# The convolution's output gate as products of summed blocks, in pairs of tiles next to other tiles

## The chip, the cores and the metric

One core of a Trainium2 chip runs the whole program. The metric is the device time of one launch in microseconds (us), the median of several runs. The engines are TensorE (PE; its weight loads, PEld, overlap the matmuls), VectorE (DVE), ScalarE (ACT), GpSimd (POOL) and SyncE (SP, which issues the DMAs). Each works through a queue of its own in order and waits for the others by semaphores.

## The reference

Two transformer blocks follow each other on a sequence of 512 positions with 1024 features. The second has two layers of mixer, cross-attention and MLP; the mixer of its layer 1 is the part that changes:

```python
def odd_mixer(h, w_in, conv_w, w_out):
    S = h.shape[1]
    proj = h @ w_in
    b_gate = proj[..., :CONV_DIM]
    c_gate = proj[..., CONV_DIM:2 * CONV_DIM]
    z = c_gate * proj[..., 2 * CONV_DIM:]
    zp = jnp.pad(z, ((0, 0), (CONV_WIDTH - 1, 0), (0, 0)))
    y = zp[:, 0:S] * conv_w[0]
    for tap in range(1, CONV_WIDTH):
        y = y + zp[:, tap:tap + S] * conv_w[tap]
    return (b_gate * y) @ w_out
...
h = h + odd_mixer(rms_norm(h, norm_mix_g[l]), conv_w_in[i], conv_w[i], conv_w_out[i])
h = h + cross_attention(rms_norm(h, norm_xattn_g[l]), mem_n, ...)
h = h + sq_relu_mlp(rms_norm(h, norm_mlp_g[l]), mlp_w1[l], mlp_w2[l])
```

CONV_DIM is 1024 and CONV_WIDTH 3; h is 512 × 1024, w_in 1024 × 3072, all float32.

## The kernel before, in words

**Layout.** Activations lie with features on the 128 partitions, eight tiles of 128 × 512 for 1024 features. A float32 matmul runs as three matmuls of type fp32r on a high and a low part of each factor (hi·hi, hi·lo, lo·hi: L2118, L2119, L2120). `t_P0H` and `t_P0L` are the parts of the normed input h, `t_P1H` and `t_P1L` those of a stage's second factor, `t_X` the residual stream.

**Weights** come in chunks of 512 KB into four buffers `t_raw`, in the order of a plan. For each chunk ACT writes the high part `t_whi` (four buffers, L2261) and DVE the low part `t_wlo` (three, L2434). A buffer `t_raw` is fetched anew once its low part is done.

**Order.** `schedule()` writes one list of steps, and each engine's program takes its own steps from it in that order; nothing is reordered later. `later()` puts a low part off to the end of the next tile (`flush()`). `row_end()` closes a norm: it splits the summed squares (DVE L2510), adds them up by a matmul with ones (PE L2200, L2201, behind the first tile of the next stage) and takes the reciprocal root (DVE L2513).

**A plain tile** (`gemm_fm`) makes 128 output columns from one chunk: 8 row blocks × 3 matmuls × 512 columns, 24 matmuls into one PSUM bank.

**The convolution** (functions `ev_c`, `ev_x`, `ev_b` in `schedule()`) runs, for m from 0 to 7, a tile of c_gate, of the third part x and of b_gate, 24 plain tiles in all. DVE evacuates them: conv_c multiplies by the squared row of the norm (L2844), conv_x multiplies in x (L2850) and runs the three taps (L2853, L2855, L2858), conv_b multiplies by the row (L2866), conv_out gates (L2869); then the product is split into P1 (ACT L2299, DVE L2490). `conv_w_out` follows as eight tiles (`mixed`), whose k-th row block needs P1's k-th tile.

**The seven products.** MLP 0 before it makes its first factor in pairs of tiles (`mlp`, `pair_of_tiles`). A pair takes two chunks as 2 × 2 blocks of 4 × 128 rows, and the input as 2 × 2 blocks of 4 row blocks × 256 columns; by the Strassen-Winograd form seven products of summed blocks give the four output blocks. A product is 4 row blocks × 3 matmuls × 256 columns. The sums of activations `T1` to `T4` are made by `combine` (a gain on ACT L2273, four DVE instructions L2455, L2456, L2459, L2462, then a split) and lie in `t_E3`; those of weights by `sums` (DVE L2444, L2445, L2447, L2449), S1 in `t_Tb`, its parts in `t_PTbR`. `Parts` splits such chunks (ACT L2268, DVE L2439). In the functions of a pair `low` writes a low part and asks for the next chunk into that buffer, `next_to` the high part of a neighbour's weights, `other` runs the neighbour's tile. `product` keeps PSUM running across products, `snap` copies a bank to SBUF (ACT L2278), `c_add` adds a bank to it (DVE L2467). Between the products stand plain tiles of a neighbour, whose weights are split into `t_MH`, `t_ML` (two pairs of buffers), while the pair's own chunks wait in `t_raw`.

Of the kernel before, what the change touches and what calls it, by code (L numbers as in the profile page):

```python
# [158 lines left out]
def schedule(T, A, plan, apart=()):  # L159
# [1791 lines left out]
    squared = [False]
    for m in range(8):
        box = {}

        def ev_c(bank, p):
            if not squared[0]:
                emit("row_squared", dst=R2, row=N.row)
                squared[0] = True
            t, free = TMP.take()
            box["t"], box["id"] = t, emit("conv_c", t=t, bank=bank, p=p, r2=R2, free=free).id  # L1960
            return "conv_c", box["id"]

        def ev_x(bank, p, m=m):
            zb = UP[:, m % 2, :]
            emit("conv_x", t=box["t"], bank=bank, p=p, z=zb[:, 16:528],
                 taps=[(zb[:, 16 - k:528 - k], gcol(f"cw{2 - k}", m)) for k in range(3)])
            return "conv_x", box["id"]
# [456 lines left out]
def vector_program(e, steps, at, mark, T):  # L2424
# [4 lines left out]
    for s in steps:  # L2429
# [408 lines left out]
        elif s.name == "conv_c":  # L2838
            for k in s.free:
                e.wait_ge(*at(*k))  # L2840
# [3 lines left out]
            e.tensor_tensor(s.t, s.bank, s.r2, ALU.mult).then_inc(*mark("conv_c", s.id))  # L2844
        elif s.name == "conv_x":
            if new(("conv_zero", 0)):
                e.wait_ge(*at("conv_zero"))
            e.wait_ge(*at("conv_c", s.id))
# [1 line left out]
            e.tensor_tensor(s.z, s.bank, s.t, ALU.mult).then_inc(*mark("conv_x", s.id))  # L2850
            e.wait_ge(*at("conv_x", s.id))
# [1 line left out]
            e.tensor_scalar(s.t, z2, c2, None, ALU.mult, ALU.bypass).then_inc(*mark("tap2", s.id))  # L2853
            e.wait_ge(*at("tap2", s.id))
            e.scalar_tensor_tensor(out=s.t, in0=z1, scalar=c1, in1=s.t, op0=ALU.mult,  # L2855
                                   op1=ALU.add).then_inc(*mark("tap1", s.id))
            e.wait_ge(*at("tap1", s.id))
            e.scalar_tensor_tensor(out=s.t, in0=z0, scalar=c0, in1=s.t, op0=ALU.mult,  # L2858
                                   op1=ALU.add).then_inc(*mark("tap0", s.id))
        elif s.name == "conv_b":  # L2860
            for k in s.free:
                e.wait_ge(*at(*k))
# [2 lines left out]
            e.wait_ge(*at(*s.p))
            e.tensor_tensor(s.s, s.bank, RB[:, :], ALU.mult).then_inc(*mark("conv_b", s.id))  # L2866
            e.wait_ge(*at("conv_b", s.id))
            e.wait_ge(*at("tap0", s.id))
            e.tensor_tensor(s.s, s.s, s.t, ALU.mult).then_inc(*mark("conv_out", s.id))  # L2869
# [212 lines left out]
```

## Time and profile before

| | us |
|---|---|
| median of 3 runs | 2223.2 (2221.88 to 2223.98) |
| the profiled execution | 2222.34, span 2220.3 |
| PE busy | 2199.0 (99%) |
| DVE busy | 1454.9 (66%) |
| ACT busy | 975.7 (44%) |
| granted PE clock, mean | 0.999 of full speed |

The span runs from the first to the last instruction that the profiler saw; 2.0 us of the execution lie around it. The window 1577 to 1705 us is the convolution, MLP 0 ends just before it. In a row of a timeline "128x512 f32<-128x512 f32" is the shape written and read, and a bracket gives the engine's idle time before the instruction and what ended it. An instruction's duration can be longer than the step to the next one, since an engine starts the next while one drains.

### The profile page before, as it was taken

The numbers are of one execution on the slowest core, as the hardware profiler recorded it, in microseconds if no ns is written. First come the engines' busy times: TensorE is split into PE (matmuls) and PEld (weight loads), VectorE is DVE, ScalarE is ACT, GpSimd is POOL, SyncE is SP. The second block draws the span as 40 slices with busy tenths as digits, with TensorE's granted clock in tenths as the row PEclk, the third lists the DMA queues.
The fourth block names the chain that finished last, engine by engine and source line by source line (L and its number), as shares of the span: only waits on it lengthen the run. The fifth ranks groups of instructions, "written<-read, shape, count | busy, mean of one in ns | idle before, by whom it ended". The sixth has DMA issues, their size and how long they took to land.

```text
span 2220.3 us, 31738 instructions
## 1 busy us (share of the span) xinstructions
PE 2199.0 (99%) x12112; PEld 1860.7 (84%) x12112; DVE 1454.9 (66%) x2448; ACT 975.7 (44%) x1676; POOL 14.5 (1%) x14
## 2 busy tenths in 40 slices
PE   9999999999999999999999999999999999999998
PEld 7877788888778888888898889998888888899997
DVE  5866565557656567686665777776755657776775
ACT  5445533334445334364553544443322435444444
POOL 0000000000000000200000000000000000000000
PEclk9999999999999999999999999999999999999999
DMA  5565443335644333465354333333233213233331
GB/s 201 164 186 156 146 129 109 104 125 180 185 135 152 116 101 115 125 176 147 114 154 132 95 95 96 114 96 105 88 99 96 89 48 105 88 102 97 99 112 55
DMA packets 136694, 268.14 MB, mean 121 GB/s; under 512 B 21773, under 2 KB 79931, under 8 KB 136160
## 3 DMA queue, kind: packets, MB, share of 16 engines
q1 hardware_dynamic: 136544, 266.13, 39.3%
...
## 4 chain that ended last, share of the span: by engine, by line
PE 70%; DVE 3%; ACT 1%; issue 1%; DMA 1%; POOL 1%; SPq 0%; DVEq 0%; POOLq 0%; ACTq 0%
PE ps L2118 22%; PE ps L2120 22%; PE ps L2119 22%; PE ps L2146 1%; PE ps L2135 1%; DVE t_wlo L2434 1%; POOL t_UP L2101 1%; DMA far<-t_UP 0%; DVE t_UP L2694 0%; PE ps L2170 0%; DVE t_Tb L2662 0%; PE ps L2158 0%; PE ps L2160 0%; PE ps L2159 0%; PE ps L2172 0%
## 5 line engine op out<-in xcount | busy, mean ns | idle before, releaser
L2118 PE MATMUL ps<-t_P0H,t_whi 128*128 128x512 f32 (+1 forms) x1568 | 590.6, 377 | 3.8 <-DVE t_P0L L2479 1.9
L2119 PE MATMUL ps<-t_P0L,t_whi 128*128 128x512 f32 (+1 forms) x1568 | 584.4, 373 | 0.0
L2120 PE MATMUL ps<-t_P0H,t_wlo 128*128 128x512 f32 (+1 forms) x1464 | 552.8, 378 | 0.0
L2434 DVE TENSOR_TENSOR t_wlo<-t_raw,t_whi 128x1024 fp32r<-128x1024 f32 (+2 forms) x289 | 342.7, 1186 | 44.7 <-PE ps L2120 32.2
L2261 ACT ACTIVATE t_whi<-t_raw 128x1024 fp32r<-128x1024 f32 (+2 forms) x295 | 300.8, 1025 | 153.6 <-PE ps L2120 152.1
L2118 PEld LDWEIGHTS ps<-t_P0H,t_whi 128*128 128x128 f32 x1568 | 295.2, 188 | 73.1 <-issue 16.4
L2119 PEld LDWEIGHTS ps<-t_P0L,t_whi 128*128 128x128 f32 x1568 | 294.9, 188 | 56.2 <-issue 1.0
L2120 PEld LDWEIGHTS ps<-t_P0H,t_wlo 128*128 128x128 f32 x1464 | 275.2, 188 | 54.7
L2118 PE MATMUL ps<-t_P1H,t_whi 128*128 128x512 f32 (+1 forms) x548 | 210.0, 383 | 1.6 <-DVE t_P1L L2819 1.0
L2119 PE MATMUL ps<-t_P1L,t_whi 128*128 128x512 f32 (+1 forms) x548 | 208.5, 380 | 0.0
L2120 PE MATMUL ps<-t_P1H,t_wlo 128*128 128x512 f32 (+1 forms) x524 | 201.1, 384 | 0.0
L2119 PE MATMUL ps<-t_P1L,t_MH 128*128 128x512 f32 x384 | 150.7, 393 | 0.0
L2120 PE MATMUL ps<-t_P1H,t_ML 128*128 128x512 f32 x384 | 150.6, 392 | 0.0
L2118 PE MATMUL ps<-t_P1H,t_MH 128*128 128x512 f32 x384 | 150.2, 391 | 0.0
L2831 DVE TENSOR_TENSOR t_X<-ps,t_X 128x512 f32<-128x512 f32 (+1 forms) x136 | 88.8, 655 | 74.0 <-PE ps L2120 73.9
L2268 ACT ACTIVATE t_whi<-t_raw 128x1024 fp32r<-128x1024 f32 x72 | 75.8, 1055 | 109.4 <-DVE t_raw L2449 109.4
L2118 PEld LDWEIGHTS ps<-t_P1H,t_whi 128*128 128x128 f32 x548 | 103.2, 188 | 22.9 <-DVE t_P1L L2819 1.2
L2119 PEld LDWEIGHTS ps<-t_P1L,t_whi 128*128 128x128 f32 x548 | 103.1, 188 | 20.8 <-issue 0.2
L2120 PEld LDWEIGHTS ps<-t_P1H,t_wlo 128*128 128x128 f32 x524 | 98.4, 188 | 20.9
L2414 ACT ACTIVATE t_TMP<-t_TMP 128x512 f32<-128x512 f32 x64 | 40.2, 628 | 136.6 <-DVE t_TMP L2827 136.6
L2287 ACT ACTIVATE t_P0H<-t_X,t_gv 128x512 fp32r<-128x512 f32 x56 | 40.3, 725 | 113.7 <-DVE t_X L2600 100.7
L2342 ACT ACTIVATE t_Tb<-t_Tb,t_ST 128x128 f32<-128x128 f32 (+3 forms) x96 | 51.6, 539 | 86.7 <-DVE t_ST L2670 73.0
...
## 6 DMA issues: line engine op xcount, KB each, us to landing
...
```

Source lines behind the costliest of these rows:

```text
L2101: e.tensor_tensor(dst, a, b, ALU.add).then_inc(*mark("window", (s.g, i)))
L2118: e.matmul(s.out, s.sh, s.mh, start=s.first, stop=False, skip_group_check=again)
L2119: e.matmul(s.out, s.sh, s.ml, start=False, stop=False, skip_group_check=again)
L2120: i = e.matmul(s.out, s.sl, s.mh, start=False, stop=s.end, skip_group_check=again)
L2135: i = e.matmul(bank[:, o:o + n], q, k, start=True, stop=True)
L2261: e.activation(s.dst, s.raw, ACT.Copy).then_inc(*mark("hi", s.j))
L2268: e.activation(s.hi, s.src, ACT.Copy).then_inc(*mark("part_hi", s.id))
L2287: e.activation(s.dst, s.src, ACT.Copy, scale=s.col).then_inc(*mark("norm_hi", s.id))
L2342: i = e.activation(t[:, o:o + n], t[:, o:o + n], ACT.Exp, bias=s.s[:, 4 + c + k:5 + c + k], accum_out=s.s[:, 8 + c + k:9 + c + k])
L2414: e.activation(s.t, s.t, ACT.Square).then_inc(*mark("relu_square", s.id))
L2434: e.tensor_tensor(s.dst, s.raw, s.hi.bitcast(F32), ALU.subtract).then_inc(*mark("lo", s.j))
L2831: e.tensor_tensor(s.x, s.bank, s.x, ALU.add).then_inc(*mark("add_x", s.id))
```

## The change

The eight b_gate tiles become four pairs of seven products, and the order of the convolution is written anew. Six plain tiles come first (c0, x0, c1, x1, c2, x2). Next to the pairs stand the other ten: c3, x3, c4 in pair 0, x4, c5, x5 in pair 1, c6, x6 in pair 2, c7, x7 in pair 3. Within a pair the order on PE is: B11, B21, the first neighbour, T2, T3, the second neighbour if there are three, T1, the last neighbour, B22, T4. The sums of activations are made from the end of MLP 0 on: sum 0 and 1 around its last two tiles, 2 and 3 between plain tiles. The convolved y(m) waits in the places of `t_P1L` (`t_QKV` lies over them) until `gate_out` multiplies it into a snapshot in SBUF. The last pair gives its buffers back to `conv_w_out`'s weights.

The core of the diff:

```diff
         if l == 0:
-            run(second(7))
+            tread[0] = "product", prods[0] - 1
+            for m in range(8):
+                if m % 2 == 0:
+                    w = Weight(chunk("mlp_w2", l, halves(512 * 7, 4), halves(128 * m, 2)))
+                run(second_tile(7, m, w, m % 2))
+                combine(*{5: ["gain 0", "gain 1"], 6: ["add 0"], 7: ["high 0", "add 1"]}.get(m, []))
...
-        def ev_b(bank, p, m=m):
-            s, free = TMP.take()
-            emit("conv_b", s=s, t=box["t"], bank=bank, p=p, free=free, row=N.row)
-            TMP.give(box["t"], ("conv_out", m))
-            split_into(P1, m, s, ("conv_out", m), give=s)
-            return "conv_b", m
-
-        for base, ev in ((1024, ev_c), (2048, ev_x), (0, ev_b)):
-            w = Weight(chunk("conv_w_in", 0, halves(0), halves(base + 128 * m, 1)))
-            run(gemm_fm(P0, w, parts8(), ev))
...
+        def gate_out(m, t, after):
+            emit("conv_b", m=m, s=t, t=y(m), after=after, row=N.row)
+            split_into(P1, m, t, ("conv_out", m), give=t)
...
+        kinds = {"c": (1024, gate_in), "x": (2048, taken_in)}
+        first = [("c", 0), ("x", 0), ("c", 1), ("x", 1), ("c", 2), ("x", 2)]
+        beside = [[("c", 3), ("x", 3), ("c", 4)], [("x", 4), ("c", 5), ("x", 5)], [("c", 6), ("x", 6)],
+                  [("c", 7), ("x", 7)]]
+        wf = [Weight(w_in(kinds[g][0], m)) for g, m in first]
...
+        def next_to(q, i):
+            if not dry and q < 4 and i < len(beside[q]):
+                U[q][f"w{i}"] = Parts(raw_of(B[q, i]), [landed(B[q, i])], MHs, MLs)
+
+        def low(q, name, of=None):
+            if not dry and name in U[q]:
+                key = U[q][name].rest()
+                if of is not None:
+                    fetch(of + NRAW, key)
+
+        def other(q, i):
+            g, m = beside[q][i]
+            run(gemm_fm(P0, U[q][f"w{i}"], parts8(), kinds[g][1](m)))
+
+        def plain(i, *work):
+            g, m = first[i]
+            run(gemm_fm(P0, wf[i], parts8(), kinds[g][1](m)))
+            combine(*work)
+
+        plain(0, "low 0", "high 1", "gain 2")
+        plain(1, "low 1", "add 2", "gain 3")
+        plain(2, "high 2", "add 3")
+        plain(3, "low 2", "high 3")
+        u0(0)
+        plain(4, "low 3")
+        low(0, "u0")
+        sums(0)
+        u12(0, 0)
+        plain(5)
+        low(0, "u1", A[0][0])
+        u12(0, 1)
+        low(0, "u2", A[0][1])
+        next_to(0, 0)
+        u3(0)
+        low(0, "w0", B[0, 0])
...
+            p = product(bx, u["u0"], 0, "B11", True, xf)
+            s1 = snap(a0, p, af)
+            if q == 0:
+                low(0, "u3")
+            next_to(q, 1)
+            p = product(bz, u["u0"], 4, "B21", True, zf)
+            u["u0"].done(p)
+            c11 = add(a0, z, s1, p)
+            PB.give(bz, c11)
+            low(q, "w1", B[q, 1])
+            other(q, 0)
+            if more:
+                u0(q + 1)
+            else:
+                ahead(W["n"] - 1)
+            p = product(bx, u["u1"], 0, "T2", False, [s1])
+            s2 = snap(b0, p, bf)
+            low(q + 1, "u0")
+            p7 = product(bv, u["u2"], 0, "T3", True, vf)
+            sums(q + 1)
+            if three:
+                next_to(q, 2)
+                other(q, 1)
+                low(q, "w2", B[q, 2])
+            u12(q + 1, 0)
+            if not more:
+                ahead(W["n"] - 1)
+            p = product(bx, u["u3"], 0, "T1", False, [s2])
+            u["u3"].done(p)
+            U[4]["S1"] = p
+            s3 = snap(b1, p)
+            c22 = add(b1, v, s3, p7)
+            low(q + 1, "u1", A[q + 1][0] if more else None)
+            other(q, 2 if three else 1)
+            next_to(q + 1, 0)
+            u3(q + 1)
+            p = product(bx, u["u1"], 4, "B22", False, [s3])
+            u["u1"].done(p)
+            c12 = snap(a1, p)
+            PB.give(bx, c12)
+            u12(q + 1, 1)
+            gate_out(2 * q, tA, [c11, c12])
+            if not more:
+                ahead(W["n"] - 1)
+            p = product(bv, u["u2"], 4, "T4", False, [c22])
+            u["u2"].done(p)
+            c21 = add(b0, v, s2, p)
+            PB.give(bv, c21)
+            low(q + 1, "u3")
+            low(q + 1, "w0", B[q + 1, 0] if more else None)
+            low(q + 1, "u2", A[q + 1][1] if more else None)
+            gate_out(2 * q + 1, tB, [c22, c21])
```

Below stand the places in the listing of DVE's and PE's instructions on which the prediction rests. A row names the line, the operation, what it writes from what it reads, and the semaphores it waits on. In the changed kernel every line of the programs stands 210 lower (L2434 is L2644, L2439 is L2649, L2200 is L2410).

The first place is DVE around the last residual add of MLP 0 (`t_X`) and the split of the summed squares (`t_P1L<-t_SQ,t_P1H`); `t_E_85` is `t_E3` with the sums of activations. Before:

```order
L2831 TENSOR_TENSOR t_X<-ps,t_X 128x512 [waits s_mm]
L2479 SCALAR_TENSOR_TENSOR t_P0L<-t_X,t_gv,t_P0H 128x512 [waits s_norm_hi]
L2487 TENSOR_TENSOR t_SQ<-t_SQ,t_TMP 128x512 [waits s_add_square,s_square]
L2833 MEMSET t_UP 128x2x16
L2434 TENSOR_TENSOR t_wlo<-t_raw,t_whi 128x1024 [waits s_mm,s_hi]
L2510 TENSOR_TENSOR t_P1L<-t_SQ,t_P1H 128x512 [waits s_norms_act]
```

and in the change:

```order
L3041 TENSOR_TENSOR t_X<-ps,t_X 128x512 [waits s_mm]
L2665 TENSOR_TENSOR t_E_85<-t_TMP 128x256 [waits s_parts_act,s_product]
L2666 SCALAR_TENSOR_TENSOR t_E_85<-t_X,t_gv,t_TMP 128x256
L2669 SCALAR_TENSOR_TENSOR t_E_85<-t_X,t_gv,t_E_85 128x256 [waits s_parts_dve]
L2672 SCALAR_TENSOR_TENSOR t_E_85<-t_X,t_gv,t_E_85 128x256 [waits s_parts_dve]
L2689 SCALAR_TENSOR_TENSOR t_P0L<-t_X,t_gv,t_P0H 128x512 [waits s_norm_hi]
L2697 TENSOR_TENSOR t_SQ<-t_SQ,t_TMP 128x512 [waits s_add_square,s_square]
L3043 MEMSET t_UP 128x2x16
L2644 TENSOR_TENSOR t_wlo<-t_raw,t_whi 128x1024 [waits s_mm,s_hi]
L2720 TENSOR_TENSOR t_P1L<-t_SQ,t_P1H 128x512 [waits s_norms_act]
```

Four instructions came in behind this residual add, and the same four behind the one before it.

The second place is DVE at the end of the sixth plain tile, x2, whose conv_x is L3058; the first tile next to pair 0, c3, reads `t_ML` (before, b_gate's tile came behind such a conv_x, and DVE's next row was an ordinary low part):

```order
L3058 TENSOR_TENSOR t_UP<-ps,t_QKV 128x512 [waits s_mm,s_conv_dve]
L3061 TENSOR_SCALAR t_QKV<-t_UP,t_gv 128x512 [waits s_conv_dve]
L3063 SCALAR_TENSOR_TENSOR t_QKV<-t_UP,t_gv,t_QKV 128x512 [waits s_conv_dve]
L3066 SCALAR_TENSOR_TENSOR t_QKV<-t_UP,t_gv,t_QKV 128x512 [waits s_conv_dve]
L2649 TENSOR_TENSOR t_TbR<-t_raw,t_whi 128x1024 [waits s_parts_act,s_mm]
L2649 TENSOR_TENSOR t_wlo<-t_raw,t_whi 128x1024 [waits s_parts_act,s_mm]
L2649 TENSOR_TENSOR t_ML<-t_raw,t_MH 128x1024 [waits s_mm,s_parts_act]
L2649 TENSOR_TENSOR t_PTbR<-t_Tb,t_PTbR 128x512 [waits s_parts_act,s_product]
L2677 TENSOR_TENSOR t_TMP<-t_TMP,ps 128x256 [waits s_product,s_parts_act]
```

The low part of c3's weights, `t_ML`, stands behind conv_x with its taps and two other low parts.

The third place is DVE in pair 0 behind the tile x3, with the low part for c4 (`t_ML`):

```order
L2659 TENSOR_TENSOR t_raw<-t_raw 128x512 [waits s_parts_dve]
L3058 TENSOR_TENSOR t_UP<-ps,t_QKV 128x512 [waits s_mm,s_conv_dve]
L3061 TENSOR_SCALAR t_QKV<-t_UP,t_gv 128x512 [waits s_conv_dve]
L3063 SCALAR_TENSOR_TENSOR t_QKV<-t_UP,t_gv,t_QKV 128x512 [waits s_conv_dve]
L3066 SCALAR_TENSOR_TENSOR t_QKV<-t_UP,t_gv,t_QKV 128x512 [waits s_conv_dve]
L2649 TENSOR_TENSOR t_ML<-t_raw,t_MH 128x1024 [waits s_parts_act,s_mm]
L2677 TENSOR_TENSOR t_TMP<-t_TMP,ps 128x256 [waits s_product,s_parts_act]
L2649 TENSOR_TENSOR t_wlo<-t_raw,t_whi 128x1024 [waits s_parts_act,s_product]
L3052 TENSOR_TENSOR t_QKV<-ps,t_UP 128x512 [waits s_mm]
```

It stands behind x3's conv_x. PE asks for both low parts at a tile's first matmul; between the end of x2 and c3's first matmul it has two products. Of PE's rows there, the last of B21 and the first three of c3:

```order
L2328 MATMUL ps<-t_P0H,t_whi 128x256
L2329 MATMUL ps<-t_P0L,t_whi 128x256
L2330 MATMUL ps<-t_P0H,t_wlo 128x256
L2328 MATMUL ps<-t_P0H,t_MH 128x512 [waits s_parts_dve,s_conv_dve]
L2329 MATMUL ps<-t_P0L,t_MH 128x512
L2330 MATMUL ps<-t_P0H,t_ML 128x512
```

Before, PE's next row behind a conv_x tile was the first of a gate tile, with 512 columns from `t_whi`.

## Rows read from the trace of the kernel before

**Rows 1.** The head of the page: span, busy time of each engine

```profile
span 2220.3 us, 31738 instructions
PE 2199.0 (99%) x12112; PEld 1860.7 (84%) x12112; DVE 1454.9 (66%) x2448; ACT 975.7 (44%) x1676; POOL 14.5 (1%) x14
```

**Rows 2.** Windows: us, then busy us (instructions) by engine, PEclk, DMA share, GB/s

```profile
940.00:944.00 4.00, 2.12 (x12) 1.55 (x12) 3.65 (x16) 2.89 (x10) 0.00 (x0) 1.00 0.07 19
1491.20:1512.20 21.00, 21.00 (x135) 18.96 (x134) 15.11 (x23) 9.10 (x14) 0.00 (x0) 1.00 0.36 102
1577.00:1705.00 128.00, 128.00 (x554) 103.87 (x553) 71.02 (x86) 28.64 (x31) 0.00 (x0) 1.00 0.31 95
...
2213.80:2215.30 1.50, 0.00 (x0) 0.00 (x0) 1.42 (x2) 0.00 (x0) 0.00 (x0) 0.97 0.00 0
2215.30:2220.00 4.70, 0.00 (x0) 0.00 (x0) 1.00 (x2) 0.00 (x0) 0.00 (x0) 0.50 0.65 225
```

**Rows 3.** Timeline of PE in MLP 0: start us, us, line, operation, out<-in

```profile
1307.15 0.28 PE L2118 MATMUL ps<-t_P0H,t_whi 128*128 128x256 f32 x1
...
1309.98 0.39 PE L2118 MATMUL ps<-t_P1H,t_MH 128*128 128x512 f32 x1
```

**Rows 4.** Timeline of DVE at the end of MLP 0

```profile
1569.10 0.68 DVE L2831 TENSOR_TENSOR t_X<-ps,t_X 128x512 f32<-128x512 f32 x1
1570.57 0.75 DVE L2479 SCALAR_TENSOR_TENSOR t_P0L<-t_X,t_gv,t_P0H 128x512 fp32r<-128x512 f32 x1 [0.79 <-ACT t_P0H L2287]
1571.24 0.69 DVE L2487 TENSOR_TENSOR t_SQ<-t_SQ,t_TMP 128x512 f32<-128x512 f32 x1
1571.85 0.68 DVE L2831 TENSOR_TENSOR t_X<-ps,t_X 128x512 f32<-128x512 f32 x1
...
1574.63 1.19 DVE L2434 TENSOR_TENSOR t_wlo<-t_raw,t_whi 128x1024 fp32r<-128x1024 f32 x1
1575.74 0.69 DVE L2510 TENSOR_TENSOR t_P1L<-t_SQ,t_P1H 128x512 fp32r<-128x512 f32 x1
```

**Rows 5.** Timeline of DVE, one sum of activations ahead of MLP 0

```profile
1225.29 0.42 DVE L2455 TENSOR_TENSOR t_E<-t_TMP 128x256 f32<-128x256 f32 x1
1225.62 0.48 DVE L2456 SCALAR_TENSOR_TENSOR t_E<-t_X,t_gv,t_TMP 128x256 f32<-128x256 f32 x1
...
1226.94 1.22 DVE L2434 TENSOR_TENSOR t_wlo<-t_raw,t_whi 128x1024 fp32r<-128x1024 f32 x1
```

**Rows 6.** Timeline of DVE in the convolution: conv_x and its taps, conv_b, conv_out

```profile
1583.10 0.69 DVE L2850 TENSOR_TENSOR t_UP<-ps,t_TMP 128x512 f32<-128x512 f32 x1
...
1585.81 1.22 DVE L2434 TENSOR_TENSOR t_wlo<-t_raw,t_whi 128x1024 fp32r<-128x1024 f32 x1
1588.63 0.69 DVE L2866 TENSOR_TENSOR t_TMP<-ps,t_RB 128x512 f32<-128x512 f32 x1 [1.61 <-PE ps L2120]
1589.36 0.69 DVE L2869 TENSOR_TENSOR t_TMP<-t_TMP 128x512 f32<-128x512 f32 x1
```

**Rows 7.** Timeline of DVE, low parts of weights in MLP 0

```profile
1302.36 1.22 DVE L2439 TENSOR_TENSOR t_ML<-t_raw,t_MH 128x1024 fp32r<-128x1024 f32 x1
1303.49 0.69 DVE L2439 TENSOR_TENSOR t_PTbR<-t_Tb,t_PTbR 128x512 fp32r<-128x512 f32 x1
```

**Rows 8.** Timeline of PE, the first matmul behind that gate tile

```profile
1588.36 0.39 PE L2118 MATMUL ps<-t_P0H,t_whi 128*128 128x512 f32 x1
```

**Rows 9.** Timeline of all engines, PE going on after a wait for DVE

```profile
1043.68 0.69 DVE L2600 SCALAR_TENSOR_TENSOR t_X<-ps,t_X 128x512 f32<-128x512 f32 x1
...
1044.42 0.50 PE L2118 MATMUL ps<-t_P1H,t_whi 128*128 128x512 f32 x1 [0.60 <-DVE t_X L2600]
...
1044.76 0.39 PE L2119 MATMUL ps<-t_P1L,t_whi 128*128 128x512 f32 x1
```

**Rows 10.** Timeline of PE, the row sum after the first convolution tile

```profile
1576.75 0.39 PE L2200 MATMUL ps<-t_P1H,t_ones 128*128 128x512 f32 x1
```

**Rows 11.** Timeline of ACT, a snapshot of a product in MLP 0

```profile
1303.17 0.39 ACT L2278 ACTIVATE t_TMP<-ps 128x256 f32<-128x256 f32 x1 [2.57 <-PE ps L2120]
```

More of the change, by code:

```diff
@@ L1641, in combine @@
                 emit("combine", t=u.t, of=u.id, x=X[:, k + 4, :], col=gcol(u.gain, k + 4), T=both,
-                     read=("x_values", ids["x_values"]))
+                     read=tread[0])
                 TMP.give(u.t, ("combined", u.id))
@@ L1942, in n1 @@
         norm_tile(m, o, "mix1", P0, sqa)
+        if m > 3:
+            tsum[m - 4] = Rec(gain="mix1", x=o)
     mlp(0, n1)
     row_end()
-    R2 = E3[:, 8, :]
+    R2 = UP[:, 2, 0:512]
     emit("conv_zero", dst=UP[:, 0:2, 0:16])
[L1951 to L1967, printed above, removed]
-        def ev_b(bank, p, m=m):
-            s, free = TMP.take()
-            emit("conv_b", s=s, t=box["t"], bank=bank, p=p, free=free, row=N.row)
-            TMP.give(box["t"], ("conv_out", m))
-            split_into(P1, m, s, ("conv_out", m), give=s)
-            return "conv_b", m
-        for base, ev in ((1024, ev_c), (2048, ev_x), (0, ev_b)):
-            w = Weight(chunk("conv_w_in", 0, halves(0), halves(base + 128 * m, 1)))
-            run(gemm_fm(P0, w, parts8(), ev))
@@ L1979, in schedule @@
+    conv()
     flush()
-    cuts = split_kv(1, [k for _, f in blocks.idle + grouped.idle + turned.idle for k in f])
+    cuts = split_kv(1, [k for _, f in blocks.idle + grouped.idle + turned.idle for k in f] +
+                    ([] if dry else [("product", prods[0] - 1)]))
     for n, _ in enumerate(mixed("conv_w_out", 0, halves(0), 1.0, "xa1", P1)):
@@ L2847, in vector_program @@
                 e.wait_ge(*at("conv_zero"))
[L2848 removed]
+            e.wait_ge(*at("conv_c", s.m))
             e.wait_ge(*at(*s.p))
[L2850 to L2851 removed]
+            e.tensor_tensor(s.z, s.bank, s.t, ALU.mult).then_inc(*mark("conv_x", s.m))
+            e.wait_ge(*at("conv_x", s.m))
             (z2, c2), (z1, c1), (z0, c0) = s.taps
[L2853 to L2854 removed]
+            e.tensor_scalar(s.t, z2, c2, None, ALU.mult, ALU.bypass).then_inc(*mark("tap2", s.m))
+            e.wait_ge(*at("tap2", s.m))
             e.scalar_tensor_tensor(out=s.t, in0=z1, scalar=c1, in1=s.t, op0=ALU.mult,
[L2856 to L2857 removed]
+                                   op1=ALU.add).then_inc(*mark("tap1", s.m))
+            e.wait_ge(*at("tap1", s.m))
             e.scalar_tensor_tensor(out=s.t, in0=z0, scalar=c0, in1=s.t, op0=ALU.mult,
[L2859 removed]
+                                   op1=ALU.add).then_inc(*mark("tap0", s.m))
         elif s.name == "conv_b":
[L2861 to L2862 removed]
             if new(s.row):
                 e.wait_ge(*at(*s.row))
[L2865 to L2869, printed above, removed]
+            for k in s.after:
+                e.wait_ge(*at(*k))
+            e.tensor_tensor(s.s, s.s, RB[:, :], ALU.mult).then_inc(*mark("conv_b", s.m))
+            e.wait_ge(*at("conv_b", s.m))
+            e.wait_ge(*at("tap0", s.m))
+            e.tensor_tensor(s.s, s.s, s.t, ALU.mult).then_inc(*mark("conv_out", s.m))
         elif s.name == "final_sums":
```

116 lines of the change are left out of this document (112 added, 4 removed).

## The prediction

> **What bounds the kernel now.** I read the head of the page first [rows 1]: TensorE (PE) is busy for 2199.0 of 2220.3 us, VectorE (DVE) for two thirds. So time goes down only if PE has less to do, and every us in which PE waits goes onto the total. Then the table by windows [rows 2], for the stretches that the change touches: in a pair of MLP 0, which already runs the seven-product scheme, PE is busy 21.00 of 21.00 us, in the convolution 128.00 of 128.00. There is no idle time on PE to win there: the change wins matmul time alone, and whatever waits it brings are new. Then the timeline of each engine where the change adds work, to see by how much DVE is ahead of PE. The profiled execution took 2222.34 us, 0.9 below the median of 2223.2; I work in differences and put them on the median.
>
> **Matmul time.** Eight gate tiles of 24 matmuls of 512 columns go: 192. In the convolution 554 such matmuls take 128.00 us [rows 2], 0.231 each: 44.4 us. Four pairs of 7 products × 4 row blocks × 3 matmuls of 256 columns come: 336. In MLP 0 two products, 24 matmuls, run from 1307.15 to 1309.98 [rows 3], 0.118 each: 39.6 to 39.8 us. **−4.7 us** (−4.5 to −5.0). The other 16 tiles keep their matmuls; the bytes of weights are the same.
>
> **What DVE gets, and where PE then waits.** Each engine works through its instructions in the order of the listing, so a late DVE instruction holds everything behind it. DVE has time enough over the stage (71.02 of 128.00 us busy [rows 2]); what counts is eight places where a thing PE needs stands behind a thing that becomes possible only late. I walked the new order with steps (start to start on a busy DVE) from the trace: 0.61 for a two-operand op on 512 columns and 0.67 for the three-operand form [rows 4]; 1.65 for the four of an activation sum, 0.33 for one 256-column add [rows 5]; 2.71 for conv_x with its taps, 0.73 for conv_b [rows 6]; 1.13 for the low part of a weight chunk, 1.22 until its end [rows 7]. DVE begins 0.27 after PE's next tile has begun (1588.63 after 1588.36 [rows 6, 8]). PE goes on 0.05 after DVE ends, and its first matmul costs 0.1 more (1043.68+0.69=1044.37, next 1044.42, then 1044.76 in place of 1044.65 [rows 9]).
>
> (a) *Row sums after the first convolution tile.* Two activation sums now stand on DVE around the last add_x of MLP 0. Back to back from 1569.10 [rows 4]: add_x 0.61, sum 1.65, norm_lo 0.67, square 0.61, add_x 0.61, sum 1.65, norm_lo 0.67, square 0.61, weight low 1.13, then the split of the sums, 0.69: 1578.0. PE takes the row sum at 1576.75 [rows 10]; before, that split ended at 1576.43. Wait 1.3+0.1 = **1.4**.
>
> (b) *First tile next to pair 0 (c3).* PE is there 24 matmuls of 0.118 = 2.84 after T0, the end of plain tile x2. Its weights' low part stands on DVE behind conv_x(2), which needs that same tile's end, and behind two more low parts: 0.27+2.71+2×1.13+1.22+0.05 = 6.51. Wait 3.67+0.1 = **3.8**.
>
> (c) *Third tile next to pair 0 (c4).* From the end of x3, PE has one product, 12×0.118 = 1.42. The low part stands behind x3's conv_x: 0.27+2.71+1.22+0.05 = 4.25. **2.9**.
>
> (d) *First tile next to pair 1 (x4).* From the end of c4, PE has four products, 5.68. ScalarE's snapshot of B22 is there at about 2.1 (1.42, 0.27, and 0.39 for the snapshot [rows 11]); DVE then does conv_b 0.73, conv_out 0.61, the last add 0.33, the sum's low part 0.61 and the chunk's 1.22: 5.65. Just in time; a weight chunk that lands late would make it up to 1. I take **0.5**.
>
> (e) *Third tile next to pair 1 (x5)*, behind c5's conv_c: 0.27+0.61+1.22+0.05 = 2.15 against 1.42: **0.85**.
>
> (f), (g) *First tiles next to pairs 2 and 3*, as (d) but behind conv_x(5) and conv_x(6): 0.27+2.71+0.73+0.61+0.33+0.61+1.22+0.05 = 6.53 against 5.68: **0.95** each.
>
> (h) *First tile of conv_w_out.* It needs the seventh activation 2.84+18×0.231 = 7.0 after x7's end. DVE, from there: 0.27, conv_x 2.71, gate 6 0.73+0.61, a weight low 1.13, the add 0.33, gate 7 0.73+0.61, the split 0.69, and 0.05: 7.86. **1.0**.
>
> Sum 1.4+3.8+2.9+0.5+0.85+0.95+0.95+1.0 = **12.35**. The shortest I can make it is b, c and half of the rest, 9.5; with d in full and another 0.5 of late landings, 13.5.
>
> **What I cost at nothing.** ScalarE's added high parts and snapshots: it is busy 28.64 of 128 us in the stage [rows 2]. The sums of the plain stretch (two more activation sums and four low parts between tiles of 5.5 us) and the sums of weights: DVE has 5.5×(1−71.02/128.00) = 2.5 us free per tile there; without that cover they would join a or b. DMA: same bytes, at 0.31 of its share [rows 2]; a chunk that is asked for late shows up in d. conv_b from SBUF in place of PSUM: same size, same price.
>
> **−4.7 + 12.35 = +7.65: 2230.9 us.** With −5.0 and 9.5 it is 2227.7, with −4.5 and 13.5 2232.2: the forecast's own range is 2227.7 to 2232.5.
>
> **Rivals.**
> 1. *All waits hidden* (a low part is moved ahead by the wait that I misread, DVE is earlier than walked): only the matmuls count, 2223.2−4.7 = 2218.5, faster. For it: MLP 0 does the same scheme with PE at 21.00 of 21.00 us. Against: there the low part of a neighbour's weights stands ahead of the long evacuations; here conv_x (b, c) waits for a tile that PE finishes only 2.84 and 1.42 before its need, and 2.71 alone exceeds the second. It decides if b and c are both below 1 us. Chance 0.04.
> 2. *Only the two long waits are real*; the six short ones lie within what a walk with mean steps can miss. 2223.2−4.7+6.7 = 2225.2, no change. Chance 0.16.
> 3. *PE's clock falls in the long wait (b).* Between 940 and 944 PE is busy 2.12 of 4.00 us and the granted clock stays 1.00; after its last matmul it is 0.97 until 2215.3 and 0.50 behind that [rows 2], the lower of its two levels (1.2 of 2.4 GHz). A wait of 3.8 lies between. If it falls, matmuls of 0.231 take 0.46 until it returns: from nothing to a whole tile's 5.5 us; half of it, 2.8, gives 2233.7. Chance 0.12. The Trainium skill (TensorE: Matmul & The Clock Gate, Part 1) says that an engine that has been idle is set back to half clock; by that rule this rival is the likelier the longer b is, and the end of the trace agrees with the 0.50 above. It speaks against any change that buys matmuls with waits.
>
> A sign change needs over 7.6 of my 12.35 us to be false; b and c alone are worth 6.7 and rest on the two longest chains. **Chances:** forecast 0.68, rival 3 0.12, rival 2 0.16, rival 1 0.04. A measurement of this kernel tells some 0.2%, 4.45 us, from no change: below 2218.75 is faster, above 2227.65 slower. So slower 0.80 (forecast and rival 3), same 0.16, faster 0.04. The range takes in rival 2 and reaches to 2234.5 for rival 3: 2225.0 to 2234.5; rival 1, the upper half of rival 3 and errors of the walk are left out, under 0.2 together.
>
> **What would show it.** In the changed profile PE's busy time is 4 to 5 us shorter, and its idle time 12 longer: at the row-sum matmul, released by DVE's split of the sums, about 1.4; at the first matmul of a tile that reads the neighbour's weights (tile MH), released by DVE's low part (tile ML), 3.8 and 2.9 in pair 0, below 1 in later pairs; at the first conv_w_out tile, released by the split into P1, about 1. MLP 0's pairs and everything from the cross-attention on keep their length. Wrong would be: no idle over 1 us at MH; a granted clock under 0.9 behind b (rival 3); idle released by a DMA or by ScalarE's high parts; or products slower than 0.118 a matmul.

## The result and the profile after

| | before | changed |
|---|---|---|
| median of 5 runs, us | 2223.77 (2221.88 to 2224.30) | 2231.76 (2228.73 to 2235.63) |
| ratio | | 1.0039, 95% interval 1.0026 to 1.0053 |
| profiled execution, its span, us | 2222.34, 2220.3 | 2231.76, 2230.0 |

The ratio is taken over all runs and is not the quotient of the two medians. By the medians the change makes the kernel 8.0 us slower, and the whole interval lies above 1. The forecast was 2230.9 with a range of 2225.0 to 2234.5. Head of the page of the changed kernel, against [rows 1]:

```profile
span 2230.0 us, 32161 instructions
PE 2198.6 (99%) x12256; PEld 1866.6 (84%) x12256; DVE 1486.9 (67%) x2504; ACT 991.9 (44%) x1708; POOL 14.5 (1%) x14
```

PE's busy time is shorter by 0.4 us only, where 4 to 5 were forecast; why, the windows below show. First the waits. These are all the instructions of PE from MLP 0's end to conv_w_out that stood still for over 0.2 us (timeline of PE, changed kernel; the last bracket is the idle time and what ended it), and behind them conv_w_out's first matmul:

```profile
1578.07 0.47 PE L2410 MATMUL ps<-t_P1H,t_ones 128*128 128x512 f32 x1 [1.19 <-DVE t_P1L L2720]
1613.21 0.47 PE L2328 MATMUL ps<-t_P0H,t_MH 128*128 128x512 f32 x1 [3.68 <-DVE t_ML L2649]
1633.01 0.47 PE L2328 MATMUL ps<-t_P0H,t_MH 128*128 128x512 f32 x1 [2.76 <-DVE t_ML L2649]
1661.89 0.47 PE L2328 MATMUL ps<-t_P0H,t_MH 128*128 128x512 f32 x1 [0.59 <-DVE t_ML L2649]
1674.01 0.47 PE L2328 MATMUL ps<-t_P0H,t_MH 128*128 128x512 f32 x1 [0.82 <-DVE t_ML L2649]
1695.93 0.47 PE L2328 MATMUL ps<-t_P0H,t_MH 128*128 128x512 f32 x1 [0.71 <-DVE t_ML L2649]
1714.07 0.40 PE L2328 MATMUL ps<-t_P1H,t_whi 128*128 128x512 f32 x1
1719.26 0.51 PE L2328 MATMUL ps<-t_P1H,t_whi 128*128 128x512 f32 x1 [0.90 <-DVE t_P1L L2700]
```

In order these are the places a, b, c, e, f, g and h of the prediction; d has none. The idle time counts from the end of the matmul before, which lies 0.16 behind the moment at which the next one normally starts (0.39 long at a step of 0.23, or 0.28 at 0.12). So each place costs 0.16 more than its idle time: 1.34, 3.84, 2.92, 0.75, 0.98, 0.88 and 1.07, together 11.8 us. The first matmul behind each wait is slow as well (the next starts 0.31 to 0.35 behind it in place of 0.23), 0.6 us over the seven.

DVE's timeline in front of the longest, b (changed kernel), is the queue that the prediction walked: conv_x of the tile x2, the third of its taps, two low parts, and only then the one PE waits for.

```profile
1606.88 0.69 DVE L3058 TENSOR_TENSOR t_UP<-ps,t_QKV 128x512 f32<-128x512 f32 x1
...
1608.91 0.75 DVE L3066 SCALAR_TENSOR_TENSOR t_QKV<-t_UP,t_gv,t_QKV 128x512 f32<-128x512 f32 x1
1609.58 1.22 DVE L2649 TENSOR_TENSOR t_TbR<-t_raw,t_whi 128x1024 fp32r<-128x1024 f32 x1
1610.71 1.22 DVE L2649 TENSOR_TENSOR t_wlo<-t_raw,t_whi 128x1024 fp32r<-128x1024 f32 x1
1611.85 1.22 DVE L2649 TENSOR_TENSOR t_ML<-t_raw,t_MH 128x1024 fp32r<-128x1024 f32 x1
```

Then the windows of the changed kernel (columns as in [rows 2]): the plain stretch, the stretches around b and c with half a us behind each, the stage from the row sum to conv_w_out.

```profile
1577.00:1606.00 29.00, 27.93 (x120) 22.69 (x121) 26.18 (x34) 7.94 (x9) 0.00 (x0) 1.00 0.25 73
1610.00:1613.00 3.00, 0.00 (x0) 0.00 (x0) 3.00 (x4) 0.73 (x2) 0.00 (x0) 1.00 0.35 70
1613.00:1616.00 3.00, 2.79 (x8) 2.31 (x9) 1.00 (x3) 0.00 (x0) 0.00 (x0) 0.66 0.98 335
1614.50:1615.00 0.50, 0.50 (x3) 0.40 (x2) 0.00 (x0) 0.00 (x0) 0.00 (x0) 0.50 0.88 336
1616.00:1620.00 4.00, 4.00 (x16) 3.14 (x16) 1.23 (x1) 2.01 (x2) 0.00 (x0) 0.82 0.22 90
1632.00:1640.00 8.00, 6.99 (x24) 5.64 (x25) 2.33 (x3) 1.30 (x2) 0.00 (x0) 0.79 0.42 131
1635.00:1635.50 0.50, 0.50 (x3) 0.41 (x2) 0.00 (x0) 0.00 (x0) 0.00 (x0) 0.50 1.05 418
1578.00:1714.00 136.00, 127.36 (x698) 110.44 (x699) 96.42 (x129) 42.09 (x58) 0.00 (x0) 0.97 0.29 90
```

Two things are to be seen. DVE is busy 26.18 of 29 us in the plain stretch. And the granted clock, 1.00 while PE stands still, falls behind b and again behind c. Matmul by matmul (timeline of PE behind b):

```profile
1613.75 0.42 PE L2330 MATMUL ps<-t_P0H,t_ML 128*128 128x512 f32 x1
1613.98 0.61 PE L2328 MATMUL ps<-t_P0H,t_MH 128*128 128x512 f32 x1
1614.39 0.63 PE L2329 MATMUL ps<-t_P0L,t_MH 128*128 128x512 f32 x1
...
1616.95 0.61 PE L2329 MATMUL ps<-t_P0L,t_MH 128*128 128x512 f32 x1
1617.38 0.41 PE L2330 MATMUL ps<-t_P0H,t_ML 128*128 128x512 f32 x1
1617.63 0.39 PE L2328 MATMUL ps<-t_P0H,t_MH 128*128 128x512 f32 x1
```

From 1613.98 to 1617.38 eight of them start 0.43 apart and not 0.23, at the lower level (1.2 GHz); behind c it is eight again. These sixteen cost 3.1 us. They count as busy PE time, which is most of why that time fell so little. (The 3.75 us in the expectations below is about these 3.1 and the 0.6 above together, and their 1.9 for one fall is 1.6.)

**The account.** From the row sum to conv_w_out's first matmul the stage took 1705.12−1576.75 = 128.4 us before and 1714.07−1578.07 = 136.0 now, +7.6; with a ahead of it and h behind, +10.0. Of that 11.8 are waits, 0.6 the first matmuls behind them and 3.1 the clock; the rest, −5.5, is what the products save. (A later run, with eight plain tiles first, shows these −5.5 alone.) The spans differ by 9.7, the medians by 8.0; the interval of the ratio is 5.8 to 11.8 us.

### The profile page after: what moved, and what is told of

The parts are those of the page before. It is cut to its first block and busy times, and to the rows that moved or that the text cites. A ratio compares the mean times of both kernels' runs of the same rounds, so it can differ in the third digit from the quotient of the medians.

```text
span 2230.0 us, 32161 instructions
## 1 busy us (share of the span) xinstructions
PE 2198.6 (99%) x12256; PEld 1866.6 (84%) x12256; DVE 1486.9 (67%) x2504; ACT 991.9 (44%) x1708; POOL 14.5 (1%) x14
## 5 line engine op out<-in xcount | busy, mean ns | idle before, releaser
L2328 PE MATMUL ps<-t_P0H,t_whi 128*128 128x512 f32 (+1 forms) x1472 | 547.7, 372 | 2.8 <-DVE t_wlo L2644 1.4
L2329 PE MATMUL ps<-t_P0L,t_whi 128*128 128x512 f32 (+1 forms) x1472 | 541.6, 368 | 0.0
L2330 PE MATMUL ps<-t_P0H,t_wlo 128*128 128x512 f32 (+1 forms) x1348 | 503.2, 373 | 0.0
L2644 DVE TENSOR_TENSOR t_wlo<-t_raw,t_whi 128x1024 fp32r<-128x1024 f32 (+2 forms) x270 | 319.3, 1183 | 44.4 <-PE ps L2330 30.5
L2328 PEld LDWEIGHTS ps<-t_P0H,t_whi 128*128 128x128 f32 x1472 | 277.4, 188 | 66.5 <-issue 16.6
L2471 ACT ACTIVATE t_whi<-t_raw 128x1024 fp32r<-128x1024 f32 (+2 forms) x277 | 281.4, 1022 | 105.7 <-PE ps L2330 102.5
L2329 PEld LDWEIGHTS ps<-t_P0L,t_whi 128*128 128x128 f32 x1472 | 277.1, 188 | 49.9 <-issue 1.0
L2330 PEld LDWEIGHTS ps<-t_P0H,t_wlo 128*128 128x128 f32 x1348 | 253.6, 188 | 47.9
L2649 DVE TENSOR_TENSOR t_ML<-t_raw,t_MH 128x1024 fp32r<-128x1024 f32 x58 | 70.7, 1220 | 46.3 <-ACT t_MH L2478 46.3
L2329 PE MATMUL ps<-t_E3R,t_whi 128*128 128x256 f32 x336 | 94.3, 281 | 0.0
```

The costliest lines, as they stand in the source:

```text
L2328: e.matmul(s.out, s.sh, s.mh, start=s.first, stop=False, skip_group_check=again)
L2329: e.matmul(s.out, s.sh, s.ml, start=False, stop=False, skip_group_check=again)
L2330: i = e.matmul(s.out, s.sl, s.mh, start=False, stop=s.end, skip_group_check=again)
L2471: e.activation(s.dst, s.raw, ACT.Copy).then_inc(*mark("hi", s.j))
L2644: e.tensor_tensor(s.dst, s.raw, s.hi.bitcast(F32), ALU.subtract).then_inc(*mark("lo", s.j))
L2649: e.tensor_tensor(s.lo, s.src, s.hi.bitcast(F32), ALU.subtract).then_inc(*mark("part_lo", s.of))
```

## The experiments

Each median stands beside that of the kernel before, measured together with it, and is followed by the ratio with its 95% interval. The diffs are against the changed kernel unless the text says otherwise; `...` marks what is left out.

**Half of the longest wait.** The low part of c3's weights goes ahead of that of u2.

```diff
         low(0, "u1", A[0][0])
+        next_to(0, 0)
+        low(0, "w0", B[0, 0])
         u12(0, 1)
         low(0, "u2", A[0][1])
-        next_to(0, 0)
         u3(0)
-        low(0, "w0", B[0, 0])
```

Expected: 

> Only the order of three steps changes: the low part of c3's weights stands on DVE ahead of that of u2, not behind it, so it comes 1.13 us earlier. Theory A (the waits come from DVE's order, and a wait of about three us also costs PE its full clock for a while): the wait at c3 falls from 3.84 to 2.7 us, the clock still falls behind it as it did behind the wait of 2.92 at c4; time 2231.8 - 1.1 = 2230.6. Theory B (the clock falls only in waits over three us and c4's fall is left over from the first): the clock stays 1.00 behind c3, 1.9 us more are won, 2228.7. Theory C (the wait is set by something else, a landing or ScalarE): wait 3.8 as before, 2231.8.

Measured: 2231.02 beside 2223.45, ratio 1.0035 (1.0022 to 1.0048). The wait at c3 is 2.71 (idle 2.55), a low part's 1.13 shorter, and the clock falls all the same (timeline of PE and two windows of this run):

```profile
1612.29 0.47 PE L2328 MATMUL ps<-t_P0H,t_MH 128*128 128x512 f32 x1 [2.55 <-DVE t_ML L2649]
```

```profile
1612.00:1614.00 2.00, 1.71 (x5) 1.42 (x6) 2.00 (x4) 0.00 (x0) 0.00 (x0) 0.69 0.93 260
1614.00:1616.00 2.00, 2.00 (x6) 1.52 (x6) 0.21 (x1) 0.00 (x0) 0.00 (x0) 0.50 0.98 350
```

So the place in DVE's queue sets the wait (theory C is out), and the clock falls behind a wait of under three us too (B is out). In time alone the run can't be told from the change.

**Without b.** The parts of c3's weights are made ahead of pair 0's sums, a tile earlier.

```diff
         plain(4, "low 3")
+        next_to(0, 0)
         low(0, "u0")
+        low(0, "w0", B[0, 0])
         sums(0)
...
-        next_to(0, 0)
         u3(0)
-        low(0, "w0", B[0, 0])
```

Expected: 

> The parts of c3's weights are made ahead of the sixth plain tile. Theory A: no wait at c3 and no fall of the clock there, the wait of 2.9 at c4 and the fall behind it stay: 2231.8 - 3.84 - 1.9 = 2226.0. Waits alone (the clock costs nothing of its own): 2231.8 - 3.84 = 2227.9. Theory D (the work is only moved and PE waits as long at the next place, T2 with the low part of u1): 2231.8.

Measured: 2229.33 beside 2223.45, 1.0027 (1.0016 to 1.0037): 2 to 3 us won where 5.8 were expected. The wait at c3 is gone, but a new one of 2.52 us stands at the second neighbour, x3 (timeline of PE), and the clock falls behind it too:

```profile
1622.14 0.47 PE L2328 MATMUL ps<-t_P0H,t_MH 128*128 128x512 f32 x1 [2.36 <-DVE t_ML L2649]
```

Theory D is right for that much: b had covered part of another wait, whose chain the run after next shows. In the change the low part of x3's weights was done at 1619.49 (timeline of DVE, changed kernel):

```profile
1618.26 1.23 DVE L2649 TENSOR_TENSOR t_ML<-t_raw,t_MH 128x1024 fp32r<-128x1024 f32 x1 [4.26 <-ACT t_MH L2478]
```

Without b PE would have been there at some 1617.7 (an estimate: 1606.52, where x2 ended, 48 matmuls of 0.118 and 24 of 0.230). So some 1.8 us of wait lay hidden behind b, at a ninth place that the prediction does not list.

**Without b, c and e.** As in the run just shown, and the third neighbour's low part ahead of the evacuation:

```diff
                 next_to(q, 2)
+                low(q, "w2", B[q, 2])
                 other(q, 1)
-                low(q, "w2", B[q, 2])
```

Expected: 

> As the run before, and the low parts of the third neighbours (c4, x5) stand on DVE ahead of the evacuation of the tile before them. Theory A: the waits of 2.92 and 0.75 go too, and with the last long wait the second fall of the clock: 2231.8 - 3.84 - 2.92 - 0.75 - 2 x 1.9 = 2220.5, granted clock 1.00 all through the convolution. Waits alone: 2224.3. Theory D: 2231.8.

Measured: 2225.43 beside 2223.45, 1.0010 (1.0002 to 1.0019). c and e are gone. The wait at x3 (2.32) stays, with one fall of the clock (1.6 us of slow matmuls), and the one at pair 1's first neighbour, d, appears with 1.22; a, f, g and h are as they were. At d it is the case that the prediction names, a weight chunk that lands late: ScalarE's high part of x4's weights waits for it and holds up the snapshot behind it (timeline of ACT).

```profile
1637.65 1.06 ACT L2478 ACTIVATE t_MH<-t_raw 128x1024 fp32r<-128x1024 f32 x1 [6.21 <-DMA t_raw<-in_wts]
...
1639.14 0.36 ACT L2488 ACTIVATE t_TMP<-ps 128x256 f32<-128x256 f32 x1
```

**All eight places.** Beside these edits, sum 1 (its later steps too, not shown) goes behind the first convolution tile (a), the low part of a pair's first neighbour ahead of the gates of the pair before (d, f, g), and in the last pair x7 ahead of T1 (h).

```diff
-                combine(*{5: ["gain 0", "gain 1"], 6: ["add 0"], 7: ["high 0", "add 1"]}.get(m, []))
+                combine(*{5: ["gain 0", "gain 1"], 6: ["add 0"], 7: ["high 0"]}.get(m, []))
...
+            if not more:
+                other(q, 1)
             p = product(bx, u["u3"], 0, "T1", False, [s2])
...
             next_to(q + 1, 0)
+            low(q + 1, "w0", B[q + 1, 0] if more else None)
             u3(q + 1)
```

Expected: 

> All eight places: also the second activation sum goes behind the first convolution tile, the low part of the next pair's first neighbour goes ahead of the gates, and the last pair runs x7 ahead of T1. Theory A: no wait over 0.3 us in the convolution, 2220.5 less 1.34, 0.98, 0.88 and 1.07 = 2216.2 if the matmuls save what they seem to (5.4 us in the trace of the change); with my 4.7 from before, 2223.8 - 4.7 = 2219.1. Theory E (the products themselves save nothing, since they also wait a little at each bank or weight): 2223.8, as before.

Measured: 2224.89 beside 2223.45, 1.0005 (0.9996 to 1.0014): no change from before, 6 to 9 us above what I expected. The waits b to h are gone; what is left are these (timeline of PE, over 0.2 us):

```profile
1578.89 0.47 PE L2413 MATMUL ps<-t_P1H,t_ones 128*128 128x512 f32 x1 [0.97 <-DVE t_P1L L2723]
1623.24 0.77 PE L2331 MATMUL ps<-t_P0H,t_MH 128*128 128x512 f32 x1 [4.60 <-DVE t_ML L2652]
1706.57 0.39 PE L2331 MATMUL ps<-t_P0H,t_whi 128*128 128x256 f32 x1 [0.47 <-ACT t_TMP L2491]
```

The one at x3 has grown to 4.76, and its chain can be read from DVE's, SP's and ACT's timelines of this run: the low part of u2, 1613.12 to 1614.34; the fetch into the buffer that it leaves, 1614.37; that chunk lands for the high part of x3's weights at 1620.69, 6.3 us later; then the low part.

```profile
1613.12 1.22 DVE L2652 TENSOR_TENSOR t_wlo<-t_raw,t_whi 128x1024 fp32r<-128x1024 f32 x1
...
1621.87 1.22 DVE L2652 TENSOR_TENSOR t_ML<-t_raw,t_MH 128x1024 fp32r<-128x1024 f32 x1 [6.60 <-ACT t_MH L2481]
```

```profile
1614.37 0.33 SPq L2276 DMA_DIRECT2D t_raw<-in_wts  x1
```

```profile
1620.69 1.06 ACT L2481 ACTIVATE t_MH<-t_raw 128x1024 fp32r<-128x1024 f32 x1 [8.48 <-DMA t_raw<-in_wts]
```

So a low part moved ahead of u2's pushes u2's back, and with it the fetch of the chunk after: u2's begins 4.2 us behind the end of x2 in the change, 5.2 in the two runs without b, 5.8 here. What is moved inside pair 0 comes out at its second neighbour. Of the growth from 2.32 to 4.76 these 0.6 are one part; the other 1.8 is the landing, which took 4.5 in the run before and 6.3 here, and why is open. The 0.47 at the end is new: with x7 ahead of T1, B22 stands right behind T1, whose snapshot it needs. And a did not go with one sum moved, since the split of the summed squares now waits for ScalarE (timeline of DVE), whose high part of them stands behind that of sum 0 and that of a chunk:

```profile
1578.06 0.69 DVE L2723 TENSOR_TENSOR t_P1L<-t_SQ,t_P1H 128x512 fp32r<-128x512 f32 x1 [0.45 <-ACT t_P1H L2526]
```

**PE kept busy in the waits.** 24 matmuls of 256 columns into an unused bank ahead of c3's tile and of c4's.

```diff
+            if q == 0:
+                keep_busy(8)
             other(q, 0)
...
+            if q == 0:
+                keep_busy(8)
             other(q, 2 if three else 1)
```

Expected: 

> The change as it is, and 24 matmuls of 256 columns (2.8 us) into an unused bank ahead of c3's tile and 24 ahead of c4's, so that PE works through most of both long waits; their results are not used. Theory A (the clock falls because PE stands still, and its fall costs time of its own): the tiles begin when they did, the granted clock stays 1.00 behind both, and the 3.75 us of slow matmuls of the change's trace are won: 2231.8 - 3.75 = 2228.0. Theory F (the fall has another cause, or costs nothing because PE would wait later anyway): 2231.8. If the extra matmuls outlast the waits: up to 0.3 us slower than that.

Measured: 2229.17 beside 2222.74, 1.0028 (1.0019 to 1.0037). The windows behind both places have a clock of 1.00 throughout:

```profile
1606.00:1612.00 6.00, 5.46 (x46) 5.26 (x45) 5.89 (x8) 3.74 (x5) 0.00 (x0) 1.00 0.19 35
1612.00:1618.00 6.00, 5.73 (x26) 4.82 (x27) 1.98 (x4) 2.01 (x2) 0.00 (x0) 1.00 0.65 230
1628.00:1638.00 10.00, 10.00 (x64) 8.98 (x63) 4.40 (x6) 1.84 (x5) 0.00 (x0) 1.00 0.35 107
```

The DVE queue is that of the change, and PE doing work that nobody needs makes the stage shorter: 132.9 us from the row sum to conv_w_out (1577.13 to 1710.02) in place of 136.0. So PE's standing still caused the falls, and these had a price of their own, 3.1 us in the trace and some 2.4 in the ratios (0.0011; the two intervals overlap, and the two kernels were not measured together).

**The activation sums later.** None at MLP 0's end, all four between the plain tiles.

```diff
-                combine(*{5: ["gain 0", "gain 1"], 6: ["add 0"], 7: ["high 0", "add 1"]}.get(m, []))
...
-        plain(0, "low 0", "high 1", "gain 2")
-        plain(1, "low 1", "add 2", "gain 3")
-        plain(2, "high 2", "add 3")
-        plain(3, "low 2", "high 3")
+        plain(0, "gain 0", "gain 1")
+        plain(1, "add 0", "gain 2")
+        plain(2, "high 0", "add 1", "gain 3")
+        plain(3, "low 0", "high 1", "add 2")
         u0(0)
-        plain(4, "low 3")
+        plain(4, "low 1", "high 2", "add 3")
+        combine("low 2", "high 3", "low 3")
```

Expected: 

> Only the activation sums move: none at MLP 0's end, all four between the plain tiles, one tile later each. Theory G (DVE is full in the six plain tiles, it is busy 26.2 of the 29 us from 1577 to 1606 in the change's trace, so what is moved in there comes out at the pair): the wait at the row sum goes (-1.34), the wait at c3 or at T2 grows by up to two sums and a split, 3 to 5 us: 2231.8 - 1.3 + 3 to 5 = 2233.5 to 2235.5. My sum before the result (DVE has 2.5 us free per plain tile): 2231.8 - 1.34 = 2230.5.

Measured: 2236.49 beside 2222.74, 1.0056 (1.0042 to 1.0070). The wait at the row sum is gone, and pair 0 pays for it (timeline of PE, and a window in the second of these waits):

```profile
1608.22 0.36 PE L2328 MATMUL ps<-t_P0H,t_whi 128*128 128x256 f32 x1 [1.59 <-DVE t_wlo L2649]
1617.16 0.76 PE L2328 MATMUL ps<-t_P0H,t_MH 128*128 128x512 f32 x1 [5.97 <-DVE t_ML L2649]
```

```profile
1612.00:1616.00 4.00, 0.00 (x0) 0.00 (x0) 3.93 (x6) 2.69 (x5) 0.00 (x0) 0.90 0.13 11
```

Beyond a matmul's usual step these are 1.76 and 6.13, in place of 3.84. Theory G: DVE is full in the six plain tiles, and my 2.5 free us per tile were not there.

**Eight plain tiles first.** c3 and x3 become plain tiles, each pair has two neighbours, the sums spread over the plain tiles, pair 0's parts are ready ahead of the eighth tile's evacuation; d, f, g as above; in the last pair PE's order is T2, x7, T1, T3, B22, T4.

```diff
-        first = [("c", 0), ("x", 0), ("c", 1), ("x", 1), ("c", 2), ("x", 2)]
+        first = [("c", 0), ("x", 0), ("c", 1), ("x", 1), ("c", 2), ("x", 2), ("c", 3), ("x", 3)]
...
+        beside = [[("c", m), ("x", m)] for m in range(4, 8)]
...
+        plain(0, "gain 0")
+        plain(1, "add 0", "gain 1")
+        plain(2, "high 0", "add 1", "gain 2")
+        plain(3, "low 0", "high 1", "add 2", "gain 3")
+        plain(4, "low 1", "high 2", "add 3")
+        plain(5, "low 2", "high 3")
+        u0(0)
+        low(0, "u0")
+        sums(0)
+        u12(0, 0)
+        plain(6, "low 3")
+        low(0, "u1", A[0][0])
+        u12(0, 1)
+        low(0, "u2", A[0][1])
+        next_to(0, 0)
+        u3(0)
+        low(0, "w0", B[0, 0])
+        plain(7)
```

Expected: 

> Eight plain tiles ahead of the pairs and two neighbours per pair; the sums of activations spread over the plain tiles, none at MLP 0's end; pair 0's parts all made ahead of the eighth tile's evacuation; the next pair's first neighbour ahead of the gates; in the last pair x7, T1, T3 behind T2. Theory A with G (the waits come from a DVE queue that is full in the plain stretch and from the places in it): with two more tiles of cover no wait over 0.5 us is left in the convolution and the clock stays 1.00: 2223.5 - 5 = 2218.5, faster than before. Theory D (a wait is only moved): some wait of 2 us or more remains, 2223 or more.

Measured: 2219.12 beside 2222.74, **0.9979 (0.9971 to 0.9988)**: faster than both kernels. From the row sum to conv_w_out PE has no idle time (windows of this run):

```profile
118.00:122.00 4.00, 4.00 (x21) 4.00 (x22) 2.34 (x4) 1.37 (x2) 0.00 (x0) 0.58 0.56 148
1579.60:1702.60 123.00, 123.00 (x700) 107.68 (x700) 101.51 (x140) 44.18 (x61) 0.00 (x0) 1.00 0.34 103
```

The stage takes 1702.57−1579.66 = 122.9 us against 128.4 before: this is the −5.5 of the products, alone. The medians differ by 3.6; in the execution shown the clock falls far ahead of the convolution (the first row), which it didn't in the profiled execution of before (1.00 from 118 to 122). Of the executions with a mean granted clock of 0.999, three of this kernel took 2216.23 to 2216.88 and six of before, measured beside them, 2220.68 to 2222.16, some 5 us apart.

**Eight plain tiles, old order within the pairs.** The run just shown, with the low part of the next pair's first neighbour again behind the gates, and x7 again between T1 and B22 (not shown in the diff, which is against that run).

```diff
             next_to(q + 1, 0)
-            low(q + 1, "w0", B[q + 1, 0] if more else None)
...
             low(q + 1, "u3")
+            low(q + 1, "w0", B[q + 1, 0] if more else None)
```

Expected: 

> As the run with eight plain tiles first, with the order within the pairs as the change has it: the low part of the next pair's first neighbour stands behind the gates, and x7 between T1 and B22. Theory A (every place in the order costs by itself): waits of 0.9 to 1.0 at the first neighbours of pairs 1, 2 and 3 and of 1.07 at conv_w_out come back, 2219.1 + 2.9 + 1.1 = 2223.1. Theory H (all of the win is the two tiles of cover, and the places matter little once DVE is not full): 2219.1.

Measured: 2220.03 beside 2223.22, 0.9990 (0.9981 to 0.9999). The three waits are back (timeline of PE):

```profile
1640.51 0.47 PE L2328 MATMUL ps<-t_P0H,t_MH 128*128 128x512 f32 x1 [0.71 <-DVE t_ML L2649]
1662.39 0.47 PE L2328 MATMUL ps<-t_P0H,t_MH 128*128 128x512 f32 x1 [0.87 <-DVE t_ML L2649]
1684.22 0.47 PE L2328 MATMUL ps<-t_P0H,t_MH 128*128 128x512 f32 x1 [0.76 <-DVE t_ML L2649]
```

They cost 2.8 us. The ratios differ by 0.0011, 2.4 us, and the medians, each against before, by 0.4: over all executions the two runs can't be told apart. Of the executions with a mean clock of 0.999, seven of this run took 2219.32 to 2220.39, some 3 us above the three with eight plain tiles first; the kernel before took 2221.41 to 2221.83 in its eight here, much as it did there. The wait at conv_w_out did not come back: here the low part of conv_w_out's chunk, 1.13 of that chain, is done before x7's evacuation (timeline of DVE).

```profile
1692.61 1.22 DVE L2644 TENSOR_TENSOR t_wlo<-t_raw,t_whi 128x1024 fp32r<-128x1024 f32 x1
...
1699.70 0.69 DVE L3058 TENSOR_TENSOR t_UP<-ps,t_QKV 128x512 f32<-128x512 f32 x1 [4.70 <-PE ps L2330]
```

In the change it stood behind x7's evacuation (timeline of DVE, changed kernel):

```profile
1711.50 0.69 DVE L3058 TENSOR_TENSOR t_UP<-ps,t_QKV 128x512 f32<-128x512 f32 x1 [4.72 <-PE ps L2330]
...
1715.54 1.22 DVE L2644 TENSOR_TENSOR t_wlo<-t_raw,t_whi 128x1024 fp32r<-128x1024 f32 x1
```

So by the traces theory A holds for the places d, f and g, and h hung on that one instruction.

**Eight plain tiles, sums 0 and 1 at MLP 0's end.** Against the run with eight plain tiles first (the diff too): sums 0 and 1 as in the change, the first steps of 2 and 3 behind the third and fourth plain tile (not shown).

```diff
+                combine(*{5: ["gain 0", "gain 1"], 6: ["add 0"], 7: ["high 0", "add 1"]}.get(m, []))
```

Expected: 

> As the run with eight plain tiles first, with sums 0 and 1 of the activations made around MLP 0's last two tiles, as in the change. Theory A: the wait of 1.34 at the row sum comes back and nothing else, 2219.1 + 1.3 = 2220.4. Theory I (the early sums free DVE later on, which pays for it): 2219.1.

Measured: 2220.18 beside 2223.22, 0.9985 (0.9976 to 0.9994), 0.0006 or 1.3 us above the run with late sums; the intervals overlap. The trace has the wait of a, 1.36 us, and no other in the convolution (timeline of PE):

```profile
1581.23 0.47 PE L2417 MATMUL ps<-t_P1H,t_ones 128*128 128x512 f32 x1 [1.20 <-DVE t_P1L L2727]
```

## Why the prediction was right

**The waits**, the term on which the sign rested, came where they were put and in nearly the size: a 1.34 (1.4 forecast), b 3.84 (3.8), c 2.92 (2.9), d 0 (0.5), e 0.75 (0.85), f 0.98 and g 0.88 (0.95 each), h 1.07 (1.0); 11.8 for 12.35. The forecast has 0.1 in each place for the slow first matmul; with the 0.6 that these measured the sum is 12.4. So walking a queue that runs in order, with steps from the trace, gave each place to 0.2 us, but for d: there the walk said just in time (5.65 against 5.68), which it was, and I added 0.5 for a late chunk. That the sum agrees to 0.1 is chance: the 0.5 too much at d and 0.5 too little at the other seven cancel. (The top of the forecast's own range is loose by some tenths: d in full and 0.5 of late landings give 13.35 and 2232.1, not 13.5 and 2232.5. Nothing hangs on it.)

**The matmuls** saved 5.5, not 4.7. A matmul of 256 columns takes 0.118 as counted; the run with eight plain tiles shows the plain ones at 0.230 where the convolution of before averaged 0.232, which over the 16 tiles that stay is some 0.5. Why they step faster is not shown.

**The clock** is the step that failed: I gave its fall 0.12 and left it out of the sum. It fell at b and also at c, 3.1 us of slow matmuls. By the prediction's own sign of being wrong, a clock under 0.9 behind b, rival 3 came true beside the forecast. The reason I leaned on, that PE had stood still for 1.9 us in [rows 2] with the clock at 1.00, was one place in one execution. Rival 3 had the mechanism, for one place, at 2.8; a fall cost 1.6, and there were two. The Trainium skill (TensorE: Matmul & The Clock Gate, Part 1) says that an idle engine is set back to half clock; the 0.50 behind both waits (1614.5 to 1615.0 and 1635.0 to 1635.5) agrees.

So the direction and the range rest on waits that were forecast rightly, but that 2230.9 stands so close to 2231.76 is in part luck: in the traces −5.5+11.8+0.6+3.1 = +10.0, where I had −4.7+12.35 = +7.65; the medians then differ by 8.0, less than the traces.

**Wrong without harm:** that DVE has 2.5 us free per plain tile. That came from its mean over the old stage [rows 2]; in the changed plain stretch it is busy 26.18 of 29.00 us. Nothing in the sum rested on it, but the repair did: undoing b, c and e one after the other brought 6 us where 11.3 were expected, because pair 0's second neighbour was late too, some 1.8 us of it by the fetch behind u2's low part, which the walk had not followed, the rest because a full DVE came to u2 later. Rivals 1 and 2 are out: all seven waits are real, and the sum of the short ones (5.0) is nearly as large as what the products win.
